# Values of the whole-key branches step by step, from a ring of three steps of turned weights

## The chip, the cores and the metric

The kernel runs on one core of a Trainium2 chip. The metric is device time in microseconds (us). The core has a matrix engine (TensorE, PE in the profile, its weight loads listed apart as PEld), VectorE (DVE), ScalarE (ACT), GpSimd (POOL), and a queue on SyncE (SP) that starts most transfers. The matrix engine writes to eight accumulation banks (`ps`) of 512 float32 values per partition.

## What is computed

One inference step of a two-layer decoder: an mLSTM layer, and then a sparse attention layer (NSA), for 512 prompt rows and for 8 sequences of 4 sample rows. The attention layer has three branches. In the first (compressed) the keys are few. The other two, selected and window, are computed in one stage here: for 512 positions and up to 16 blocks of 64 both see every key up to the query's own position, so they are ordinary causal attention over 512 keys, each with its own keys and values. Of the reference this is:

```python
    s = jnp.einsum('bqghd,bgqkd->bghqk', qg, kb) * scale
    p = _masked_softmax(s, (kpos <= qpos[None, None, :, None])[:, :, None])
    o_sel = jnp.einsum('bghqk,bgqkd->bqghd', p.astype(vb.dtype), vb)
    s = jnp.einsum('bqghd,bkgd->bghqk', qg, kwin) * scale
    wmask = ((wpos[None, :] <= qpos[:, None]) & (wpos[None, :] > qpos[:, None] - WINDOW)
             & (wpos[None, :] >= 0))
    p = _masked_softmax(s, wmask)
    o_win = jnp.einsum('bghqk,bkgd->bqghd', p.astype(vwin.dtype), vwin)
    o = jnp.stack([o_cmp, o_sel, o_win], axis=2)
...
    y = (o.astype(f32) * g[..., None]).reshape(bsz, s, 3, B_ATT) * jax.nn.silu(z.astype(f32))
    y = jnp.sum(y, axis=2).astype(x.dtype) @ w_out
```

There are 16 query heads in 4 key groups of 4 heads, 64 values wide.

## The kernel before, in words

The program is a row of stages; only `stage_keys` (the selected and the window branch, lines 2380 to 2763) is touched. Each engine has its own instruction list there, and they meet by semaphores only. `stage_out`, the output projection, follows.

**Units and pairs.** A unit (`units`, 16 of them) is one branch v, one half gp of the key groups and one tile i of 128 query rows. Within a half of units i runs 0, 1, 2, 3, and tile i sees i+1 key tiles of 128, so a unit with i = 3 costs four times one with i = 0. A unit has four pairs n = 4u + hh (64 in all); a pair is two heads (`par` 0 and 1) that belong to two key groups and sit in the upper and the lower half of the partitions.

**The loop.** Every engine runs over n. In iteration n PE computes the scores of pair n (line 2475) and adds the causal mask (2479); then, in some iterations, a part of the work for the sample rows (2488 to 2532), and up to iteration 59 a part of a gate projection of a later branch (`z_blocks`, line 2160, into bank 6); then it transposes the softmax weights of pair n-1 (2544, TURN = 1). DVE takes the maxima of the scores (2648), ACT the exponential with the row sum (2615), DVE the reciprocal times the branch gate (2673, 2674), and each of the two scales one head's weights (2677 on DVE, 2634 on ACT). `keep` copies the transposed weights of pair n-1 from their bank to the tile `PT` (2453 on DVE, 2451 on ACT). `gate` finishes a gate bank (2660).

**Values.** `PT` holds the turned weights of two whole units, [2, par, key tile, hh, 128]. When all four pairs of a unit are in it, three iterations after the last one's scores (`unit_at(n, TURN + 2)`, n = 4u + 6), PE computes the unit's output at once: for each key tile and each head half one matmul of 64 weight columns (the values V) with 512 moving columns (four pairs), at the end of the iteration (2556), in bank 7. One iteration later (n = 4u + 7) DVE multiplies it with the gate `z`, at the end of its iteration (`out`, 2686); GpSimd adds it to `y` (2762). `keep` waits, at a unit's first pair, for the values of the unit two before.

Of the kernel before, what the change touches and what calls it, by code (L numbers as in the profile page):

```python
# [15 lines left out]
T = 512  # L16
NT = T // 128
# [12 lines left out]
H, DH, G = 16, 64, 4  # L30
HPG = H // G
# [95 lines left out]
def open_at(pe, k, key, bank):  # L127

    n = k.bank_turns[bank]
    if n:  # L130
        pe.wait_ge(k.bank_free[bank], n)
    k.bank_turns[bank] = n + 1
    k.bank_of[key] = (bank, n + 1)
    return k.ps[:, bank], k.bank_full[bank]
# [9 lines left out]
def drained(eng, k, key):  # L144

    bank, n = k.bank_of[key]
    eng.wait_ge(k.bank_free[bank], n)
# [2229 lines left out]
def stage_keys(nc, k, ctx):  # L2377
# [5 lines left out]
    def sb(name, shape, dt=F32):  # L2383
        return ctx.enter_context(nc.sbuf_tensor(name, shape, dt))
    TURN = 1
    P = sb("P", [128, 2, 2, T])
    PT = sb("PT", [128, 2, 2, NT, HPG, 128])
    nmx = sb("nmx", [128, 4, 2])
    sm = sb("sm", [128, NT, H])
    rc = sb("rc", [128, 2, 2])  # L2390
# [12 lines left out]
    units = [(v, i, gp) for v in range(2) for gp in range(2) for i in range(NT)]  # L2403
    pairs = [(v, i, gp, hh) for v, i, gp in units for hh in range(HPG)]
    NP, NU = len(pairs), len(units)
# [30 lines left out]
    def unit_at(n, behind):  # L2436

        n -= behind
        return n // HPG if 0 <= n < NP and n % HPG == HPG - 1 else None

    def keep(eng, n, par):
        v, i, gp, hh = pairs[n]
        u = n // HPG
        if hh == 0 and u >= 2:
            bank, c = k.bank_of[("O", u - 2)]
            eng.wait_ge(k.bank_full[bank], c)
        b, free = full_bank(eng, k, ("T", n, par))
        dst = PT[:, u % 2, par, 0:i + 1, hh, :]
        src = b[:, 0:128 * (i + 1)].rearrange("p (j q) -> p j q", q=128)
        if par:  # L2450
            eng.activation(dst, src, ACT.Copy).then_inc(free, 1)
        else:
            eng.tensor_copy(dst, src).then_inc(free, 1)
# [10 lines left out]
    def _(pe):  # L2464
        z_features(pe, k, 1, 0)
        for n in range(STEPS):
# [14 lines left out]
            for a in range(2):  # L2481
                q = two(n, KEYS[a])
# [55 lines left out]
            if TURN <= n < NP + TURN:  # L2538
                i = pairs[n - TURN][1]
                for par in range(2):  # L2540
# [2 lines left out]
                    for j in range(i + 1):  # L2543
                        m = pe.transpose(b[:, 128 * j:128 * j + 128], P[:, (n - TURN) % 2, par, 128 * j:128 * j + 128], k.ident[:, :])
                    m.then_inc(full, 1)
            u = unit_at(n, TURN + 2)
            if u is not None:
                v, i, gp = units[u]
                for hh in range(HPG):
                    for par in range(2):  # L2550
                        drained(pe, k, ("T", HPG * u + hh, par))
                b, full = open_at(pe, k, ("O", u), 7)
                for j in range(i + 1):
                    for par in range(2):
                        g = 2 * gp + par
                        m = pe.matmul(b[64 * par:64 * par + 64, :], k.V[:, v, j, DH * g:DH * g + DH],
                                      PT[:, u % 2, par, j, :, :].rearrange("p h q -> p (h q)"), start=j == 0, stop=j == i)
                m.then_inc(full, 1)

    @block.sync  # L2560
    def _(sp):
# [77 lines left out]
    def _(dve):  # L2639
# [56 lines left out]
        for n in range(STEPS + 1):  # L2696
            if n in ROWS_BACK:
                add_samples(dve, k, st, ROWS_BACK[n])
            if n < NP:
                maximum(n)  # L2700
            for a in range(2):
# [44 lines left out]
            if gates_done(n) is not None:  # L2746
                bank, no = gates_done(n)
                gate(*bank, no)
            u = unit_at(n, TURN + 3)
            if u is not None:  # L2750
                out(u)

    @block.gpsimd
    def _(pool):
# [127 lines left out]
def build(nc, a, outs):  # L2882

    k = Ctx()
    with ExitStack() as ctx:
        def sb(name, shape, dt=F32, where=ctx):
            return where.enter_context(nc.sbuf_tensor(name, shape, dt))

        def sem(name):
            return ctx.enter_context(nc.semaphore(name))  # L2890
# [109 lines left out]
        k.gate_exp = sem("gate_exp")  # L3000
        k.gt_halved = sem("gt_halved")
        k.gate_done = sem("gate_done")
        k.y_ready = sem("y_ready")
        k.rows_read = sem("rows_read")
        k.xu_high = sem("xu_high")
# [122 lines left out]
```

## Time and profile before

| | us |
|---|---|
| median of 3 runs | 1504.17 (1503.64 to 1505.37) |
| the profiled execution | 1504.39 |
| its span on the core | 1502.6 |
| PE busy | 1396.2 (93%) |
| DVE busy | 743.9 (50%) |
| ACT busy | 515.8 (34%) |
| `stage_keys` loop, scores of pair 0 to the last product | 1139.0 to 1439.7 |

The span is what lies between the first and the last instruction; the profiled execution's own time adds 1.8 us around it. Matmuls are pipelined: a matmul's recorded end is modelled and lies some way behind its last column, so busy time of PE counts more than the columns. Each float32 matmul stands in the trace as two records.

### The profile page before, as it was taken

The page shows a single profiled execution, that of the slowest core. Times are in us where ns is not written, and L with a number is a line of the kernel's source. Part 1 is how long each engine was busy: PE and PEld are TensorE (multiplying, and loading weights), DVE is VectorE, ACT ScalarE, POOL GpSimd, SP SyncE. Part 2 cuts the span into 40 slices and gives each one's busy share as a digit, 9 for nine tenths or more (in the row PEclk, how much of TensorE's full clock was granted, in tenths as well). Part 3 has the DMA queues.
Part 4 walks back from the last instruction along what each step waited for, and adds up shares of the span by engine and source line. Part 5 has one row for each costly group of instructions (what it writes and reads, how often), then busy time and mean ns, then how long its engine had stood idle before and what let it go on. Part 6 is the DMA issues. An engine that isn't in the chain of part 4 may idle for free. (4 is left out here: it accounts for less than half of the span.)

```text
span 1502.6 us, 24705 instructions
## 1 busy us (share of the span) xinstructions
PE 1396.2 (93%) x9357; PEld 1002.6 (67%) x9357; DVE 743.9 (50%) x1575; ACT 515.8 (34%) x1227; POOL 189.6 (13%) x231
## 2 busy tenths in 40 slices
PE   4899899999996699999799999999999999999978
PEld 4899655454542599777577999787666555555456
DVE  4676446676755732625633231005034656565646
ACT  5232524242421332423522231122104545454542
POOL 5221041313130100000110110100000000010020
PEclk9999999999998799999899999997999999999999
DMA  6431236767677522222443340011141314141221
GB/s 188 167 113 56 72 105 225 252 221 256 222 257 261 212 84 86 85 102 87 146 170 120 102 165 11 3 60 58 57 124 33 122 52 141 60 113 63 43 93 60
DMA packets 93835, 182.06 MB, mean 121 GB/s; under 512 B 10855, under 2 KB 24835, under 8 KB 92515
## 3 DMA queue, kind: packets, MB, share of 16 engines
q1 hardware_dynamic: 90998, 164.88, 33.4%
q0 software_dynamic: 2720, 15.60, 3.1%
q8 instruction: 76, 1.25, 0.3%
q14 instruction: 41, 0.34, 0.1%
HBM read 133.82 MB, written 54.95 MB: 126 GB/s over the span
## 5 line engine op out<-in xcount | busy, mean ns | idle before, releaser
L1022 DVE SCALAR_TENSOR_TENSOR wring<-wring,nbw,ps 128x512 f32<-128x512 f32 x128 | 86.9, 742 | 59.8 <-PE ps L673 59.7
L2160 PE MATMUL ps<-xnT,wring 128*64 128x256 f32 (+1 forms) x768 | 101.3, 400 | 1.9 <-DVEq L2662 1.7
L2615 ACT ACTIVATE P<-ps,nmx 128x128 f32<-128x128 f32 (+3 forms) x128 | 66.3, 522 | 95.4 <-DVE nmx L2648 95.4
L2142 PE MATMUL ps<-xnT,wring 128*64 128x256 f32 (+1 forms) x768 | 90.4, 398 | 1.3 <-PEq L2874 1.3
L1417 PE MATMUL ps<-wh,xl 128*128 128x512 f32 x224 | 88.1, 393 | 0.0
L416 PE MATMUL ps<-xuh,wuh 128*128 128x256 f32 (+1 forms) x256 | 77.6, 303 | 11.3 <-DVE wring_low L363 10.3
L1238 PE MATMUL ps<-xh,wh 128*128 128x256 f32 (+1 forms) x256 | 75.0, 293 | 7.2 <-DVE xl L1284 7.1
L2142 PEld LDWEIGHTS ps<-xnT,wring 128*64 128x64 f32 x768 | 59.0, 139 | 32.2 <-issue 3.8
L2648 DVE TENSOR_REDUCE nmx<-ps 128x1 f32<-128x128 f32 (+3 forms) x128 | 56.8, 486 | 47.0 <-PE ps L2479 40.8
L417 PE MATMUL ps<-xul,wuh 128*128 128x256 f32 (+1 forms) x256 | 76.3, 298 | 0.0
L418 PE MATMUL ps<-xuh,wring_low 128*128 128x256 f32 (+1 forms) x256 | 76.3, 298 | 0.0
L1239 PE MATMUL ps<-xl,wh 128*128 128x256 f32 (+1 forms) x256 | 74.3, 290 | 0.0
L1240 PE MATMUL ps<-xh,wl 128*128 128x256 f32 (+1 forms) x256 | 73.9, 289 | 0.0
L2160 PEld LDWEIGHTS ps<-xnT,wring 128*64 128x64 f32 x768 | 50.9, 136 | 31.9 <-issue 8.4
L1902 PE MATMUL ps<-cRh,cwh 128*128 128x384 f32 x192 | 67.5, 352 | 0.0
L1370 DVE TENSOR_TENSOR wring_low<-wring,wh 128x512 fp32r<-128x512 f32 x64 | 41.1, 687 | 53.2 <-PE ps L1381 53.2
L1903 PE MATMUL ps<-cRl,cwh 128*128 128x384 f32 x192 | 65.4, 341 | 0.0
L1904 PE MATMUL ps<-cRh,cwl 128*128 128x384 f32 x192 | 65.4, 340 | 0.0
L2066 PE MATMUL ps<-xnT,wring 128*128 128x256 f32 (+1 forms) x256 | 60.6, 401 | 2.2 <-PEq L3096 2.2
L416 PEld LDWEIGHTS ps<-xuh,wuh 128*128 128x128 f32 x256 | 51.3, 200 | 11.8 <-issue 5.3
L2762 POOL TENSOR_TENSOR arena<-arena,tmp 128x512 f32<-128x512 f32 x16 | 20.3, 1271 | 303.5 <-DVEq L2689 303.5
L2066 PEld LDWEIGHTS ps<-xnT,wring 128*128 128x128 f32 x256 | 49.7, 195 | 12.8 <-issue 2.3
(489 smaller groups left out, 3135.3 us busy)
## 6 DMA issues: line engine op xcount, KB each, us to landing
wring<-in_state_C_dram SPq DMA_DIRECT2D x64, 512.0 KB, 5.2
out_dram<-wring SPq DMA_DIRECT2D x64, 512.0 KB, 5.3
wring<-in_a_w_up_dram SPq DMA_DIRECT2D x8, 2048.0 KB, 8.6
wring<-in_b_w_in_dram SPq DMA_DIRECT2D x8, 2048.0 KB, 9.1
wring<-in_a_w_down_dram SPq DMA_DIRECT2D x4, 2048.0 KB, 8.6
craw<-in_cache_kv_dram SPq DMA_DIRECT2D x64, 128.0 KB
arena<-in_cache_kv_dram SPq DMA_DIRECT2D x32, 256.0 KB, 3.9
arena<-in_cache_win_dram SPq DMA_DIRECT2D x8, 1024.0 KB, 6.0
```

The lines of the kernel that those rows point to most:

```text
L416: pe.matmul(b[:, 0:t1 - t0], w_hi, x_hi, start=kt == 0, stop=False)
L417: pe.matmul(b[:, 0:t1 - t0], w_hi, x_lo, start=False, stop=False)
L418: m = pe.matmul(b[:, 0:t1 - t0], w_lo, x_hi, start=False, stop=kt == KD - 1)
L1022: dve.scalar_tensor_tensor(out=c, in0=c, scalar=nbws[:, h % 2, 2 * S + s:2 * S + s + 1], in1=b[:, :], op0=ALU.mult, op1=ALU.add).then_inc( ...
L1238: pe.matmul(out, w_hi, x_hi, start=kt == 0, stop=False)
L1239: pe.matmul(out, w_hi, x_lo, start=False, stop=False)
L1240: m = pe.matmul(out, w_lo, x_hi, start=False, stop=kt == KD - 1)
L1417: m = pe.matmul(b, x_lo, w_hi, start=False, stop=last and kt == KD - 1)
L1902: pe.matmul(b[:, 0:CROW], w_hi, r_hi, start=j == 0, stop=False)
L2066: m = pe.matmul(b[:, 0:t1 - t0], w[:, kt, 128 * m4:128 * m4 + 128], k.xnT[:, kt, t0:t1], start=kt == 0, stop=kt == KD - 1)
L2142: m = pe.matmul(b[64 * par:64 * par + 64, 0:t1 - t0], w[:, kt, x:x + DH], k.xnT[:, kt, t0:t1], start=kt == 0, stop=kt == KD - 1)
L2160: m = pe.matmul(k.ps[64 * par:64 * par + 64, bank, 0:t1 - t0], w[:, kt, x:x + DH], k.xnT[:, kt, t0:t1], start=kt == 0, stop=kt == KD - 1)
```

## The change

`PT` becomes a ring of three pairs, [3, par, 512], written in one run. The values of pair n-3 are computed at the end of PE's iteration n, for that pair's heads alone: per key tile and half one matmul with 128 moving columns, into that pair's quarter of bank 7. The bank is opened at a unit's first pair and handed over at its last; for the three others a new semaphore `values_done` counts. `keep` now waits, for each pair n from 3 on, for the values of pair n-3. `out` moves from the end of DVE's iteration 4u + 7 to its start, ahead of the maxima.

```diff
--- before.py
+++ after.py
@@ -2384,7 +2384,8 @@
         return ctx.enter_context(nc.sbuf_tensor(name, shape, dt))
     TURN = 1
     P = sb("P", [128, 2, 2, T])
-    PT = sb("PT", [128, 2, 2, NT, HPG, 128])
+    SLOTS = TURN + 2
+    PT = sb("PT", [128, SLOTS, 2, T])
     nmx = sb("nmx", [128, 4, 2])
     sm = sb("sm", [128, NT, H])
     rc = sb("rc", [128, 2, 2])
@@ -2439,14 +2440,17 @@
         return n // HPG if 0 <= n < NP and n % HPG == HPG - 1 else None
 
     def keep(eng, n, par):
-        v, i, gp, hh = pairs[n]
-        u = n // HPG
-        if hh == 0 and u >= 2:
-            bank, c = k.bank_of[("O", u - 2)]
-            eng.wait_ge(k.bank_full[bank], c)
+
+        i = pairs[n][1]
+        if n >= SLOTS:
+            u, hh = divmod(n - SLOTS, HPG)
+            if hh == HPG - 1:
+                bank, c = k.bank_of[("O", u)]
+                eng.wait_ge(k.bank_full[bank], c)
+            else:
+                eng.wait_ge(k.values_done, (HPG - 1) * u + hh + 1)
         b, free = full_bank(eng, k, ("T", n, par))
-        dst = PT[:, u % 2, par, 0:i + 1, hh, :]
-        src = b[:, 0:128 * (i + 1)].rearrange("p (j q) -> p j q", q=128)
+        dst, src = PT[:, n % SLOTS, par, 0:128 * (i + 1)], b[:, 0:128 * (i + 1)]
         if par:
             eng.activation(dst, src, ACT.Copy).then_inc(free, 1)
         else:
@@ -2543,19 +2547,19 @@
                     for j in range(i + 1):
                         m = pe.transpose(b[:, 128 * j:128 * j + 128], P[:, (n - TURN) % 2, par, 128 * j:128 * j + 128], k.ident[:, :])
                     m.then_inc(full, 1)
-            u = unit_at(n, TURN + 2)
-            if u is not None:
-                v, i, gp = units[u]
-                for hh in range(HPG):
-                    for par in range(2):
-                        drained(pe, k, ("T", HPG * u + hh, par))
-                b, full = open_at(pe, k, ("O", u), 7)
+            if 0 <= n - TURN - 2 < NP:
+                o = n - TURN - 2
+                v, i, gp, hh = pairs[o]
+                if hh == 0:
+                    open_at(pe, k, ("O", o // HPG), 7)
+                for par in range(2):
+                    drained(pe, k, ("T", o, par))
                 for j in range(i + 1):
                     for par in range(2):
                         g = 2 * gp + par
-                        m = pe.matmul(b[64 * par:64 * par + 64, :], k.V[:, v, j, DH * g:DH * g + DH],
-                                      PT[:, u % 2, par, j, :, :].rearrange("p h q -> p (h q)"), start=j == 0, stop=j == i)
-                m.then_inc(full, 1)
+                        m = pe.matmul(k.ps[64 * par:64 * par + 64, 7, 128 * hh:128 * hh + 128], k.V[:, v, j, DH * g:DH * g + DH],
+                                      PT[:, o % SLOTS, par, 128 * j:128 * j + 128], start=j == 0, stop=j == i)
+                m.then_inc(k.bank_full[7] if hh == HPG - 1 else k.values_done, 1)
 
     @block.sync
     def _(sp):
@@ -2696,6 +2700,9 @@
         for n in range(STEPS + 1):
             if n in ROWS_BACK:
                 add_samples(dve, k, st, ROWS_BACK[n])
+            u = unit_at(n, TURN + 3)
+            if u is not None:
+                out(u)
             if n < NP:
                 maximum(n)
             for a in range(2):
@@ -2746,9 +2753,6 @@
             if gates_done(n) is not None:
                 bank, no = gates_done(n)
                 gate(*bank, no)
-            u = unit_at(n, TURN + 3)
-            if u is not None:
-                out(u)
 
     @block.gpsimd
     def _(pool):
@@ -3000,6 +3004,7 @@
         k.gate_exp = sem("gate_exp")
         k.gt_halved = sem("gt_halved")
         k.gate_done = sem("gate_done")
+        k.values_done = sem("values_done")
         k.y_ready = sem("y_ready")
         k.rows_read = sem("rows_read")
         k.xu_high = sem("xu_high")
```

**PE, the end of the loop.** The rows of TensorE's list from the scores of pair 61 on; lines 2475, 2479, 2544 and 2556 of before are 2479, 2483, 2548 and 2560 of the changed file. `x` counts matmuls. Before:

```order
L2475 MATMUL ps<-KT,Qp 128x512 x2
L2479 MATMUL ps<-causb,identb 128x128 x2
L2544 MATMUL ps<-ident,P 128x128 x8
L2475 MATMUL ps<-KT,Qp 128x512 x2
L2479 MATMUL ps<-causb,identb 128x128 x2
L2544 MATMUL ps<-ident,P 128x128 x8
L2556 MATMUL ps<-PT,V 64x512 x6
L2475 MATMUL ps<-KT,Qp 128x512 x2
L2479 MATMUL ps<-causb,identb 128x128 x2
L2544 MATMUL ps<-ident,P 128x128 x16
L2556 MATMUL ps<-PT,V 64x512 x8
```

And now:

```order
L2479 MATMUL ps<-KT,Qp 128x512 x2
L2483 MATMUL ps<-causb,identb 128x128 x2
L2548 MATMUL ps<-ident,P 128x128 x8
L2560 MATMUL ps<-PT,V 64x128 x6
L2479 MATMUL ps<-KT,Qp 128x512 x2
L2483 MATMUL ps<-causb,identb 128x128 x2
L2548 MATMUL ps<-ident,P 128x128 x8
L2560 MATMUL ps<-PT,V 64x128 x8
L2548 MATMUL ps<-ident,P 128x128 x8
L2560 MATMUL ps<-PT,V 64x128 x24
```

Each iteration has its values behind the transposes; the last row of before, eight matmuls of 512 columns behind the last transposes, is now the 24 of pairs 61 to 63, and those of pair 60 stand before them. The same holds for every iteration from n = 3 on.

**DVE, the last four steps' `out`.** The product of unit 14 (2686, now 2690) and the maxima of pair 63 (2648, now 2652). Before:

```order
L2648 TENSOR_REDUCE nmx<-ps 128x1 x2
L2673 RECIPROCAL rc<-sm 128x2
L2674 TENSOR_TENSOR rc<-rc,gt 128x2
L2677 TENSOR_SCALAR P<-P,rc 128x512
L2453 COPY PT<-ps 128x4x128
L2686 TENSOR_TENSOR tmp<-ps,z 128x512
L2453 COPY PT<-ps 128x4x128
L2686 TENSOR_TENSOR tmp<-ps,z 128x512
```

And now:

```order
L2690 TENSOR_TENSOR tmp<-ps,z 128x512
L2652 TENSOR_REDUCE nmx<-ps 128x1 x2
L2677 RECIPROCAL rc<-sm 128x2
L2678 TENSOR_TENSOR rc<-rc,gt 128x2
L2681 TENSOR_SCALAR P<-P,rc 128x512
L2457 COPY PT<-ps 128x512 x2
L2690 TENSOR_TENSOR tmp<-ps,z 128x512
```

The product has moved from between the last two copies to ahead of the maxima.

## Rows read from the trace of the kernel before

**Rows 1.** Busy time (us, instructions) of the engines by stretch, granted clock, DMA

```profile
1139.00:1192.00 53.00, 52.77 (x514) 29.85 (x513) 34.10 (x104) 26.55 (x86) 1.72 (x2) 1.00 0.27 81
...
1361.00:1413.00 52.00, 51.89 (x431) 26.81 (x428) 32.77 (x100) 24.67 (x83) 3.81 (x3) 1.00 0.13 46
1413.00:1427.00 14.00, 11.43 (x97) 5.64 (x97) 10.11 (x27) 8.45 (x21) 1.27 (x1) 1.00 0.52 106
```

**Rows 2.** Timeline (start, duration in us), PE and PEld around a values group

```profile
1295.85 3.65 PE L2556 MATMUL ps<-PT,V 128*64 128x512 f32 x16
...
1296.33 0.14 PEld L2556 LDWEIGHTS ps<-PT,V 128*64 128x64 f32 x2 [0.29 <-issue]
...
1296.76 0.14 PEld L2556 LDWEIGHTS ps<-PT,V 128*64 128x64 f32 x2 [0.28 <-issue]
...
1299.43 0.49 PE L2475 MATMUL ps<-KT,Qp 64*128 64x128 f32 x4
1299.85 0.11 PEld L2479 LDWEIGHTS ps<-causb,identb 128*128 128x128 bf16 x2
```

**Rows 3.** The same view, transposes and the scores behind them

```profile
1310.33 0.66 PE L2544 MATMUL ps<-ident,P 128*128 128x128 f32 x4
...
1310.92 0.70 PE L2475 MATMUL ps<-KT,Qp 64*128 64x256 f32 x4
```

**Rows 4.** The same view, values of the sample rows, 32 weight columns each

```profile
1303.93 1.08 PE L2529 MATMUL ps<-arena 128*32 128x128 f32 x32
...
1304.94 0.42 PE L2532 MATMUL ps<-V,arena 32*32 32x128 f32 x8
```

**Rows 5.** The same view, the gate projection of step 30 behind its wait

```profile
1273.49 0.71 PE L2160 MATMUL ps<-xnT,wring 128*64 128x288 f32 x4 [1.06 <-DVEq L2662]
```

**Rows 6.** Waits from 1139 to 1440 us: total us, times, longest

```profile
PE ps L2160 <- DVEq L2662: 1.7, 3, 1.1
...
PE ps L2475 <- ACT P L2615: 1.5, 2, 1.0
```

**Rows 7.** Timeline of DVE around the product `out` of unit 13

```profile
1410.80 1.02 DVE L2648 TENSOR_REDUCE nmx<-ps 128x1 f32<-128x384 f32 x2 [2.65 <-PE ps L2479]
...
1415.05 0.69 DVE L2686 TENSOR_TENSOR tmp<-ps,z 128x512 f32<-128x512 f32 x1 [0.52 <-DVEq L2662]
1416.05 1.29 DVE L2648 TENSOR_REDUCE nmx<-ps 128x1 f32<-128x512 f32 x2 [0.31 <-DVE tmp L2686]
```

**Rows 8.** Timeline of the last steps, all engines

```profile
1417.70 1.13 PE L2475 MATMUL ps<-KT,Qp 64*128 64x512 f32 x4 [0.96 <-ACT P L2615]
...
1423.48 1.28 DVE L2648 TENSOR_REDUCE nmx<-ps 128x1 f32<-128x512 f32 x2
...
1426.78 1.13 PE L2475 MATMUL ps<-KT,Qp 64*128 64x512 f32 x4
...
1427.96 1.04 PE L2544 MATMUL ps<-ident,P 128*128 128x128 f32 x8
...
1428.10 1.29 DVE L2648 TENSOR_REDUCE nmx<-ps 128x1 f32<-128x512 f32 x2 [0.77 <-PE ps L2479]
...
1431.42 1.09 PE L2544 MATMUL ps<-ident,P 128*128 128x128 f32 x8 [2.41 <-DVE P L2677]
...
1432.55 0.60 ACT L2451 ACTIVATE PT<-ps 128x512 f32<-128x512 f32 x1 [0.52 <-PE ps L2544]
1432.80 0.69 DVE L2453 COPY PT<-ps 128x512 f32<-128x512 f32 x1 [0.24 <-DVE tmp L2686]
...
1433.84 5.07 PE L2556 MATMUL ps<-PT,V 128*64 128x512 f32 x16 [1.33 <-DVE PT L2453]
...
1439.05 0.69 DVE L2686 TENSOR_TENSOR tmp<-ps,z 128x512 f32<-128x512 f32 x1 [5.56 <-PE ps L2556]
```

**Rows 9.** Busy time by stretch as in rows 1, during the last values group

```profile
1434.00:1436.00 2.00, 2.00 (x6) 0.67 (x7) 0.00 (x0) 0.00 (x0) 0.12 (x1) 0.50 0.00 0
```

## Prediction

> **What bounds the kernel now.** I read four views in this order: the busy time by stretch, the timeline of TensorE's matmuls, the list of waits, and the timeline of all engines at the end of the loop. The stage `stage_keys` with its 64 steps (pair n = 0 to 63) runs from 1139 to 1441 us. From 1139 to 1413 TensorE (PE) is busy over 98% of each stretch, at a granted clock of 1.00, while VectorE (DVE) is busy about 62% [rows 1]. So in the first 60 steps every column and every pause of PE is paid. From 1413 to 1427 PE is busy 11.4 of 14 us [rows 1]: those steps (60 to 63, four key tiles each) carry no gate projections, and the chain maximum, exponential, reciprocal, scaling sets their pace. From 1427 on, the stage hangs on one chain: transposes of pair 63, their copies, the last values chunk, its product on DVE, and the sum on GpSimd.
>
> One caution: a matmul's recorded duration holds some 0.17 us behind its last column, so I price PE work from start to start.
>
> **Part 1, four times as many values groups.** Before, one group per four steps: in step 34 it starts at 1295.85 and the scores behind it at 1299.43, 3.58 us [rows 2]. It is 16 records, two at a time (the two halves of 64 columns run together); a pair of records follows the last after 0.43 us (1296.33 to 1296.76), so the streaming is 8 x 0.427 = 3.41 us. The rest, 0.17 us, is a fixed price: the first pair takes 0.48 in place of 0.43 (0.05, weights that nothing hides), and about 0.10 to 0.12 passes at the change to the next shape. The transposes show the same: 4 records of 0.107 us are 0.43, the next shape starts 0.59 later, so 0.16 [rows 3]. I take 0.15 per group, bounds 0.14 and 0.17.
>
> Now there are 64 groups in place of 16. Each new one stands between transposes and scores, two shapes that already meet there with one change; it adds a change and a first load. Those of pairs 0 to 55 come before the scores of step 59, the last step that PE bounds: 56 against 14, so 42 x 0.15 = **+6.3 us** (5.9 to 7.1). The six left fall into the stretch where PE waits, and cost nothing as long as it does.
>
> Streaming itself: four matmuls of 128 columns in place of one of 512 are the same columns. What is not shown is 64-wide weights with 128 columns. The nearest row is narrower, values of the sample rows, 32 records, four at a time, 128 columns each: 8 x 0.107 = 0.85, and 1.01 passes to the next shape [rows 4], which leaves 0.15 or 0.16 fixed and nothing per pair. The scores of one key tile load two weights of 128 columns for each pair of 128 moving columns; their two pairs and both fixed parts take 0.42 (1299.43 to the mask matmuls at 1299.85) [rows 2]: 0.21 streaming, 0.10 first load, 0.10 change. They load twice as much per pair as the new groups and still hide the second pair's load. So 0 per pair.
>
> **Part 2, pauses of PE in the first 60 steps.** There are seven, where PE catches up with DVE or ScalarE: five times the gate projection waits until DVE has emptied its bank (the largest ends at 1273.49, [rows 5]), twice scores wait for a free bank. The waits list gives 1.7 us for the first kind and 1.5 for the second, of which 0.96 belongs to step 61 [rows 6, 8]; with 0.1 to 0.17 us hidden behind each previous matmul's recorded end, the seven are 2.9 us. Each lies in a step without a values group. Now each such step gets 0.36 us (one key tile) to 1.0 us (four), which pushes PE's need back while DVE's readiness stays, or comes earlier by the product `out` that no longer stands at an iteration's end. The 1.1 us pause keeps some 0.3. Against that, the steps before an old group lose the long break in which DVE caught up; where a group of three key tiles had stood (steps 14 and 46), DVE starts the maxima up to 0.7 us behind the scores, and the next gate projection may wait 0.2. I keep 0.6 us of pauses: **-2.3 us** (-2.9 to -1.4).
>
> **Part 3, the end.** In steps 60 to 63 PE needs 1.2 (scores and mask, 1426.78 to 1427.96) + 0.96 (transposes) + 1.0 (values) = 3.2 us a step, DVE 4.62 - 0.77 idle = 3.85 between the maxima of 62 and 63 [rows 8]. So DVE sets the pace. One `out` costs it 1.0 us, 1415.05 to 1416.05 with the pause behind it [rows 7]. Unit 13's moves ahead of the maxima of step 59, where DVE waits 2.65 us for scores [rows 7]: -0.7 from step 60 on (more is cut off by the scores of step 60). Unit 14's moves ahead of the maxima of 63, where 0.77 us was idle: +0.25. Transposes of pair 63 start 0.4 us earlier, at 1431.0 in the old count. Then, before: copies to 1433.5 (ScalarE's from 1432.55, DVE's from 1432.80, late because `out` stood ahead of it), the whole unit's values from 1433.84, recorded 5.07 us, its product at 1439.05 [rows 8]. Now: transposes until 1431.95, pairs 61 and 62 until 1433.95 while the copies of 63 run, pair 63 until 1434.85, and 0.2 to the product: 1435.05, **-4.0 us**.
>
> The clock: the old last group ran partly at 1.2 GHz (granted 0.50 from 1434 to 1436, [rows 9]) after PE had been idle 2.4 and 1.3 us with one group between [rows 8]; that cost it 5.07 - 3.65 = 1.4 us against step 34's [rows 2]. The new end still has about 2.2 us idle ahead of the last transposes, then none. Bounds 0 and 1.7; I take **+0.5**.
>
> Nothing else costs. The copies move as many elements, written in one run in place of strided; both a copy and the product of 512 elements take 0.69 us [rows 7, 8], so layout is not what limits them. The new wait of `keep` for pair n asks for the values of n-3, which PE has issued ahead of the transposes that `keep` waits for anyway. The first group of unit u now waits for `out` of u-1 at the start of the same DVE iteration; PE has scores, gate projection and transposes (over 2 us) ahead of it, so it is cover, until step 63. GpSimd's sums and what follows only shift.
>
> **Sum.** 6.3 - 2.3 - 4.0 + 0.5 = **+0.5 us**. The profiled execution took 1504.39 us, of which 1502.6 are its span; it lies 0.2 above the median of three, 1504.17. So the median becomes 1504.7. By the bounds it is -1.0 (5.9 - 2.9 - 4.0) to +3.4 (7.1 - 1.4 - 4.0 + 1.7), so 1503.2 to 1507.6.
>
> **Rivals.** (a) *Slower: DVE becomes the bound inside the loop.* Bank 7 opens for unit u only after `out` of u-1, and `out` delays the maxima of the same step by up to 0.5 us where the scores are short. If DVE runs more than 2 us behind PE at a unit's first step, PE waits there, some 0.4 us in each of 15 units: +6, 1510.7. Against: DVE waited for scores at those steps in the timeline, 2.65 us at step 59 [rows 7], and the old group's time is given to DVE in pieces, not taken. It decides from a lag of about 2 us. Chance 0.13. (b) *Slower: each weight load is paid.* If the 0.05 us of the first pair falls on every pair, 240 more pairs cost 12 us: 1516. The row of four at a time speaks against it [rows 4]. Chance 0.04. (c) *Faster: no price for the change of shape*, if small groups slip into the pauses behind transposes: only first loads, 42 x 0.05 = 2.1, so -3.7: 1500.5. Against: both the long and the short group pay it [rows 2, 3]. Chance 0.05. (d) *The end is not shortened*, because the chunk was not what the end waited for: +4.5, 1508.7. Against: DVE's 5.6 us wait for it ends at 1439.05 [rows 8]. Chance 0.04.
>
> The Trainium skill, page "TensorE: Matmul & The Clock Gate", section "The mechanism", says that a weight load overlaps running matmuls only where the row group differs. Here all groups use all 128 rows, so by that rule (b) would hold and the change would be 12 us slower; the rows of this trace disagree, since pairs in one row group follow each other at the pure streaming time.
>
> **Chances.** Forecast 0.74, (a) 0.13, (b) 0.04, (c) 0.05, (d) 0.04. 0.2% (3 us) is about what a measurement of this kernel can tell from no change. Faster by more: (c) and a little of the forecast, 0.07. Slower by more: (a), (b), (d) and the forecast's upper edge (above 1507.2), 0.23. Within: 0.70. The range of 8 in 10 is the forecast's, opened on both sides to the nearer part of (c) and (a): 1501.5 to 1509.
>
> **What would show it.** Right: 64 values groups, each about 0.15 us more than its streaming (0.36 us for one key tile, 1.0 for four); the scores of step 59 some 4 us later than 1409.69; the last product about 4.5 us after the last transposes start, against 7.6; PE's waits for DVE in the loop under 1 us. Wrong: pairs of 128 columns further apart than 0.11 us; waits of PE for `out` (bank 7); or maxima that start later than the scores by more than 1 us in most steps.

## The result

The changed kernel takes 1509.48 us (median of 8 runs, 1506.17 to 1513.38), the kernel before 1504.1 (8 runs, 1503.22 to 1506.19). The ratio is 1.0033, 95% interval 1.0019 to 1.0048: 0.2 to 0.5% slower. The forecast was 1504.7, with a range of 1501.5 to 1509.

The profiled execution of the changed kernel is the slowest of its eight, 1513.38 us; the head of its page:

```profile
span 1511.6 us, 25759 instructions
...
PEclk9899999999997899999899999988999999999979
```

I read both traces by four marks. All times are starts in the timeline, counted from the first scores of the loop (1139.01 before, 1140.37 after; what lies ahead of them is the same program in both):

| us from the first scores | before | after | difference |
|---|---|---|---|
| scores of pair 59 | 270.68 | 276.55 | +5.87 |
| transposes of pair 63 | 292.41 | 298.32 | +5.91 |
| product of the last unit | 300.04 | 305.30 | +5.26 |
| from there to the end of the span | 63.58 | 65.96 | +2.38 |

So the loss is made in the first 59 steps, steps 59 to 63 add nothing, the end gives back 0.65 us in place of 4, and the output stage, whose program is the same, took 2.4 us more in this execution. Another 1.36 us of the 9.0 between the two spans lie ahead of the first scores, where the program is the same too. In the 14 profiled executions of this case the first scores stand between 1137.7 and 1142.7 us, whatever was changed behind them, so the whole time of a single execution says less than the marks do.

**The loop.** Busy time by stretch, the columns as in [rows 1]: TensorE is still full, and now nearly so in the stretch of steps 60 to 62 as well (14.67 of 15 us), where it was busy 11.43 of 14 us.

```profile
1140.40:1193.00 52.60, 52.60 (x520) 30.95 (x518) 33.76 (x103) 26.62 (x86) 2.54 (x2) 1.00 0.27 81
...
1362.00:1417.00 55.00, 54.55 (x529) 32.26 (x529) 33.39 (x101) 25.85 (x84) 3.82 (x3) 1.00 0.13 44
1417.00:1432.00 15.00, 14.67 (x155) 8.97 (x155) 11.19 (x28) 8.39 (x21) 1.27 (x1) 1.00 0.37 75
```

The values of one pair with four key tiles, in TensorE's timeline (the answer to [rows 2]), line 2560 being the values and 2479 the scores:

```profile
1217.35 1.09 PE L2560 MATMUL ps<-PT,V 128*64 128x128 f32 x16
1218.37 0.49 PE L2479 MATMUL ps<-KT,Qp 64*128 64x128 f32 x4
```

1.02 us pass, 8 x 0.107 = 0.85 of them streaming: 0.17 per group, what the group of 3.4 us had paid once per unit.

**Pauses.** Between the first scores and those of pair 59 I add up TensorE's gaps beyond the usual 0.1 us. Before they were seven and 2.95 us; now four, at steps 15 (0.31), 30 (0.32), 40 (0.84) and 55 (0.52), and 1.99 us, all ahead of the gate projection. The largest is at step 40, where there was none. The rows are DVE's product `out` of unit 8 (2690), the maxima of pair 39, an instruction of GpSimd for the sample rows (2205), DVE's reciprocal times the branch gate (2678), the gate of iteration 39 (2664), and TensorE's wait for it:

```profile
1319.43 0.69 DVE L2690 TENSOR_TENSOR tmp<-ps,z 128x512 f32<-128x512 f32 x1
...
1320.43 0.76 DVE L2652 TENSOR_REDUCE nmx<-ps 128x1 f32<-128x256 f32 x2 [0.31 <-DVE tmp L2690]
...
1321.76 1.89 POOL L2205 TENSOR_TENSOR osall<-osall,gt 32x1024 f32<-32x1024 f32 x1
...
1322.20 1.48 DVE L2678 TENSOR_TENSOR rc<-rc,gt 128x2 f32<-128x2 f32 x1
...
1324.52 0.41 DVE L2664 SCALAR_TENSOR_TENSOR z<-masks,ps 128x256 f32<-128x256 f32 x1
...
1325.14 0.65 PE L2160 MATMUL ps<-xnT,wring 128*64 128x256 f32 x4 [0.77 <-DVEq L2666]
```

`out` and the 0.31 us behind it take 1.0 us of DVE's time ahead of the maxima. The larger loss is the product of 2 columns at 1322.20: it takes 1.48 us where its median is 0.16, and ends 0.02 us after GpSimd's instruction does. In the kernel before it is the product of step 40 that is long (0.92 us, at 1322.91), and no pause of TensorE follows there. By an estimate from these rows, with the product at 0.16 us the gate would have been ready 1.3 us earlier, before TensorE asked for it, and step 40 would have had no pause. No run moves GpSimd's instruction alone; two runs that move `out` bear on it below.

**The end.** The timeline of all engines, the answer to [rows 8]:

```profile
1422.60 1.29 DVE L2652 TENSOR_REDUCE nmx<-ps 128x1 f32<-128x512 f32 x2 [0.71 <-PE ps L2483]
...
1426.85 1.29 DVE L2652 TENSOR_REDUCE nmx<-ps 128x1 f32<-128x512 f32 x2 [0.50 <-PE ps L2483]
...
1435.38 1.29 DVE L2652 TENSOR_REDUCE nmx<-ps 128x1 f32<-128x512 f32 x2 [0.31 <-DVE tmp L2690]
...
1438.69 1.97 PE L2548 MATMUL ps<-ident,P 128*128 128x128 f32 x8 [2.42 <-DVE P L2681]
...
1440.59 4.93 PE L2560 MATMUL ps<-PT,V 128*64 128x128 f32 x48
...
1445.67 0.69 DVE L2690 TENSOR_TENSOR tmp<-ps,z 128x512 f32<-128x512 f32 x1 [5.07 <-PE ps L2560]
```

DVE waits for the scores of pairs 60 and 61 (0.71, 0.50), which it had not done before. And the last transposes and values run at half clock (1.2 in place of 2.4 GHz), as the busy time by stretch tells (granted clock in the last column but two):

```profile
1440.00:1442.00 2.00, 2.00 (x18) 1.67 (x18) 0.60 (x1) 0.60 (x1) 0.00 (x0) 0.50 0.00 0
1442.00:1444.00 2.00, 2.00 (x22) 2.00 (x20) 0.00 (x0) 0.00 (x0) 0.00 (x0) 0.50 0.00 0
...
1450.00:1452.00 2.00, 1.42 (x4) 1.17 (x5) 2.00 (x4) 2.00 (x5) 0.00 (x0) 0.50 0.16 49
```

The last row is the start of the output stage, at half clock as well.

### The profile page after: what moved, and what is told of

Same layout as the page of the kernel before. It is cut to its first block and busy times, and to the rows that moved or that the text cites. A ratio compares the mean times of both kernels' runs of the same rounds, so it can differ in the third digit from the quotient of the medians.

```text
span 1511.6 us, 25759 instructions
## 1 busy us (share of the span) xinstructions
PE 1409.1 (93%) x9837; PEld 1031.0 (68%) x9837; DVE 744.2 (49%) x1575; ACT 516.1 (34%) x1227; POOL 189.6 (13%) x231
```

## The experiments

Theory after the comparison: (T1) the loop pays a fixed price per group, for the change of tile shape and the first loads; (T2) the end would be worth its gain if the clock held. The rival to T1 is that DVE, late with gates and `out`, sets the loop's time, or that short pairs pay each weight load; to T2, that the clock has no part in the difference.

**The group beside its own shape.**

```diff
             if gates_at(n) is not None:
                 bank, (k0, k1) = gates_at(n)
                 z_blocks(pe, k, *bank, k0, k1)
+            if 0 <= n - TURN - 2 < NP:
+                ...            (the values of pair n-3, moved up)
             if TURN <= n < NP + TURN:
                 ...            (the transposes of pair n-1)
-            if 0 <= n - TURN - 2 < NP:
-                ...
```

> The changed kernel with each pair's values group moved, on TensorE alone, from behind the transposes to just behind the gate projection, which also uses 64 weight columns. Theory (the change is slow because each of 42 more groups pays about 0.16 us for a change of tile shape and a first unhidden load, in a loop that TensorE bounds): in steps 3 to 59 the group then meets its own shape, so 57 groups lose 0.16 us, 9 us against the changed kernel; some of it comes back as pauses, so 6 to 9 us less than the changed kernel and 1 to 4 us less than before, 1500 to 1503. Rival 1 (the loop is slow because DVE is late with the gate banks and `out`, not by the price of groups): the groups' place changes nothing, 1507 to 1510. Rival 2 (each weight load of a 128-column pair is paid, wherever it stands): 1507 to 1510 as well, with pairs further apart than 0.11 us in the trace.

Measured: 1501.62 us (11 runs), ratio to before 0.9983 (0.9973 to 0.9992), some 8 us less than the changed kernel. Scores of pair 59 at 269.21 in place of 276.55, with pauses of 3.11 in place of 1.99 us: 8.46 us less work for TensorE, and 56 groups stand ahead of that mark, so 0.151 us each. The timeline shows gate projection, values (2552) and transposes (2561) of step 59:

```profile
1408.51 1.19 PE L2160 MATMUL ps<-xnT,wring 128*64 128x288 f32 x8
1409.53 0.82 PE L2552 MATMUL ps<-PT,V 128*64 128x128 f32 x12
1410.29 0.88 PE L2561 MATMUL ps<-ident,P 128*128 128x128 f32 x6
```

From values to transposes pass 0.76 us for three key tiles (6 x 0.107 = 0.64 streaming): only the one change of shape, 0.1, is left. T1 holds, its rivals fall. Of the lower work the pauses took back 1.1 us. Not all of the 8 us is the loop's: the edit also puts the values of pair 61 ahead of the last transposes, and the last product follows these after 3.00 us, where the changed kernel took 6.98, partly at half clock.

**The old unit beside its own shape.**

```diff
                 z_blocks(pe, k, *bank, k0, k1)
+            u = unit_at(n, TURN + 2)
+            if u is not None:
+                ...            (the unit's values, moved up)
             if TURN <= n < NP + TURN:
```

> The kernel before with its unit-wide values group moved behind the gate projection, ahead of the transposes; nothing else. Theory (price per change of shape): 14 of the 16 groups lose 0.16 us, 2.2 us less than before, 1501.5 to 1502.5. Rival (a late transpose of up to 3.5 us makes DVE and ScalarE late): pauses of TensorE appear in the next steps, same as before or up to 3 us slower.

Scores of pair 59 at 268.70 against 270.68, with pauses 0.15 us longer: 2.13 us for 14 groups, 0.152 each, the same price from the other kernel. But the time is 1506.39 us (11 runs), ratio 1.0005 (0.9996 to 1.0014): no gain. In the profiled execution, the longest of the 11 (1509.26), half-clock stretches at the end were twice as long as before (6.8 against 3.4 us, twice) and from the last product to the end passed 66.01 us against 63.58; its first scores stood 3.7 us later than before, ahead of anything that was changed. The loop's price is as expected; the total is not, and not for the rival's reason, since the pauses hardly grew. What took the gain back in the other executions is not shown.

**Only the last unit step by step.**

```diff
-            if u is not None:
+            if u is not None and u < NU - 1:
                 ...            (values of a whole unit)
+            o = n - TURN - 2
+            if NP - HPG <= o < NP:
+                ...            (values of pair o, 128 columns, into bank 7)
...
-            if u is not None:
+            if u is not None and u != NU - 2:
                 out(u)
+            if n == NP - 1:
+                out(NU - 2)    (ahead of the maxima of pair 63)
```

> The kernel before with only the last unit (pairs 60 to 63) valued step by step, 3 more groups in place of 48, and `out` of the unit ahead of it moved to the start of step 63. Theory of the prediction: the end is 4 us shorter at full clock, 1500 to 1501. Rival, after the changed kernel's trace (the last groups run at half clock because TensorE idles 2.6 us ahead of the last transposes): about 1 us shorter on average, 1502.5 to 1504, with a wider spread over the runs than before.

1502.14 us (11 runs), ratio 0.9982 (0.9973 to 0.9991). The loop is as before (270.66). The end in this execution ran at full clock:

```profile
1430.51 1.09 PE L2544 MATMUL ps<-ident,P 128*128 128x128 f32 x8 [1.53 <-DVE P L2692]
...
1431.53 2.84 PE L2570 MATMUL ps<-PT,V 128*64 128x128 f32 x48
...
1434.52 0.69 DVE L2701 TENSOR_TENSOR tmp<-ps,z 128x512 f32<-128x512 f32 x1 [2.62 <-PE ps L2570]
```

From last transposes to last product 4.01 us, the 4.05 of the prediction's sum, against 7.63. Over the runs it is 2 us, between the two expectations. Whether the clock fell at the end of the other executions is not known; 2 us is also what the end turns out to be worth at equal clock (2.2, below).

**`out` back to the iteration's end.**

```diff
-            u = unit_at(n, TURN + 3)
-            if u is not None:
-                out(u)
             if n < NP:
                 maximum(n)
             ...
             if gates_done(n) is not None:
                 bank, no = gates_done(n)
                 gate(*bank, no)
+            u = unit_at(n, TURN + 3)
+            if u is not None:
+                out(u)
```

> The changed kernel with `out` put back to the end of DVE's iteration. Theory: the ring needs the early `out`, because bank 7 opens for the next unit in the very step at whose end `out` now stands; TensorE then waits for a whole DVE iteration every fourth step, 1 to 2 us in each of 15 units, 15 to 30 us slower than the changed kernel (1524 to 1540), and waits for bank 7 show in the list of waits. Rival (DVE keeps close enough to TensorE, and the early `out`, which stands ahead of the maxima, costs more than it gives): the same as the changed kernel or up to 3 us faster.

1544.36 us (4 runs), ratio 1.0262 (1.0246 to 1.0278), 35 us above the changed kernel. The list of waits (us in total, times, longest) has what was not there:

```profile
PEld ps L2560 <- DVEq L2692: 32.3, 15, 4.2
PE ps L2560 <- DVEq L2692: 28.7, 15, 3.9
```

15 waits for bank 7, one per unit after the first, 2.1 us each. The direction is the theory's, the size above its range. So the move of `out` belongs to the ring: it is the price of opening bank 7 three steps earlier. The pauses ahead of the gate projection at steps 15, 30 and 55 are 0.32, 0.32 and 0.52 us here too, so the early `out` is not their cause. At step 40 the pause is 0.15 us in place of 0.84, and none of the products of line 2678 is long.

**Fillers: the clock held at the end.** Matmuls without use fill TensorE's idle time; the lots are shorter than the idle time.

```diff
+def keep_awake(pe, k, count):
+    for _ in range(count):
+        pe.matmul(k.ps[:, 6, 0:128], k.ident[:, :], k.ident[:, :], start=True, stop=True)
...
+            if n == NP:
+                drained(pe, k, ("z", 2, 7, 1))
+                keep_awake(pe, k, 10)
             if TURN <= n < NP + TURN:
...
+            if n == NP + TURN + 1:     (in the kernel before only)
+                keep_awake(pe, k, 5)
...
+        keep_awake(pe, k, 11)          (behind the loop)
...
+        keep_awake(pe, k, 9)           (stage_out, ahead of its first matmul)
         hv.tiles(pe, ("o", 0), CH_OUT, 0, True, True, True, outer=True, between={24: samples})
```

> The kernel before with matmuls that compute nothing of use (128 columns against the identity, into the idle gate bank) in TensorE's idle times at the end: 10 ahead of the transposes of pair 63, 5 ahead of the last values, 11 behind them, 9 at the start of the output stage; each lot is shorter than the idle time measured there. Theory (half clock after idle time is what blurs the end): the granted clock stays 1.00 through the end of the stage, the last values take 3.7 us in place of 5.1, the first matmuls of the output stage 1.3 us in all less; 2.5 to 3.5 us less than before, 1501 to 1502, with a narrower spread. Rival (the clock falls anyway, or the fillers delay the real work): same as before or slower.

> The changed kernel with the same fillers (10, none, 11, 9). Theory: with the clock held, the 24 last short matmuls take 2.7 us in place of 4.9 and the output stage starts at full clock, so 4 to 6 us less than the changed kernel, 1503.5 to 1505.5; what is left against the kernel before with fillers is the loop's 5.9 us less the 3.5 us that the end gives: 2 to 3 us. Rival (the change's cost lies in the loop alone and the clock has no part): 1509, and 5 us or more above the kernel before with fillers.

Before with fillers: 1501.55 us (9 runs), ratio 0.9976 (0.9966 to 0.9986). Changed with fillers: 1506.12 (11 runs), ratio 1.0008 (0.9998 to 1.0018). By the ratios both gain some 3.7 us, and between them lie 4.6 us, nearly the 5.4 without fillers. The kernel before came out as its theory had it; the changed one is above its theory's 1503.5 to 1505.5 and below the rival's 1509. In both profiled executions no half clock is left from the loop on, until the last microseconds, and the marks can be compared:

| us | before, fillers | changed, fillers | difference |
|---|---|---|---|
| scores of pair 59 | 270.69 | 276.55 | +5.86 |
| transposes of pair 63 | 292.42 | 298.33 | +5.91 |
| from there to the last product | 6.22 | 4.01 | -2.21 |
| to the end of the span | 62.32 | 62.29 | -0.03 |

That is +3.67 us; of the 0.9 us that the medians have more, 0.54 lie ahead of the first scores in the two profiled executions. The timelines of the last transposes, values and product, before and changed:

```profile
1431.63 1.10 PE L2552 MATMUL ps<-ident,P 128*128 128x128 f32 x8 [0.18 <-DVE P L2688]
...
1434.06 3.65 PE L2566 MATMUL ps<-PT,V 128*64 128x512 f32 x16 [0.21 <-issue]
...
1437.85 0.69 DVE L2697 TENSOR_TENSOR tmp<-ps,z 128x512 f32<-128x512 f32 x1 [4.15 <-PE ps L2566]
```

```profile
1438.08 1.09 PE L2556 MATMUL ps<-ident,P 128*128 128x128 f32 x8
...
1439.10 2.84 PE L2568 MATMUL ps<-PT,V 128*64 128x128 f32 x48
...
1442.09 0.69 DVE L2699 TENSOR_TENSOR tmp<-ps,z 128x512 f32<-128x512 f32 x1 [2.56 <-PE ps L2568]
```

The 4.93 us of the 48 records are 2.84, so the changed end does run at the length that the prediction gave it once the clock holds. But the old group also gains (5.07 to 3.65), so at equal clock the step-by-step end is worth 2.2 us, not 4; my expectation of 2 to 3 us between the two kernels had overlooked that. T2 falls: the clock is not what makes the change slower on average. In the profiled executions without fillers the difference behind the first scores is 7.6 us in place of 3.7, and the 4 us more lie in the end and the output stage, where the half-clock stretches are.

**Fillers behind the stage only** (11 and 9, in the kernel before, none ahead of the transposes).

```diff
+        drained(pe, k, ("z", 2, 7, 1))
+        keep_awake(pe, k, 11)
...
+        keep_awake(pe, k, 9)
         hv.tiles(pe, ("o", 0), CH_OUT, 0, True, True, True, outer=True, between={24: samples})
```

> The kernel before with fillers behind the last values and at the start of the output stage only (11 and 9). It splits what the fillers gave there, 2.7 us in the profiled runs. Theory (each half-clock stretch costs what its own matmuls lose): the last product stays 7.6 us behind the last transposes, and from it to the end 62.3 us pass in place of 63.6; 1.0 to 2.0 us less than before. Rival (the clock of the output stage hangs on the idle time ahead of the last transposes too): 63.6 us or more remain.

1505.45 us (11 runs), ratio 1.0002 (0.9993 to 1.0011): nothing, though the stage's start ran at full clock. In the profiled execution another half-clock stretch stood 20 us into the output stage (64.03 us from last product to end). The rival's number holds (63.6 us or more): fillers in these places alone did not pay. Its reason, the idle time ahead of the last transposes, is not tested by it, and why that stretch comes and goes stays open.

**The width alone.**

```diff
-                for j in range(i + 1):
-                    for par in range(2):
-                        g = 2 * gp + par
-                        m = pe.matmul(b[64 * par:64 * par + 64, :], k.V[:, v, j, DH * g:DH * g + DH],
-                                      PT[:, u % 2, par, j, :, :].rearrange("p h q -> p (h q)"), start=j == 0, stop=j == i)
+                for hh in range(HPG):
+                    for j in range(i + 1):
+                        for par in range(2):
+                            g = 2 * gp + par
+                            m = pe.matmul(b[64 * par:64 * par + 64, 128 * hh:128 * hh + 128], k.V[:, v, j, DH * g:DH * g + DH],
+                                          PT[:, u % 2, par, j, hh, :], start=j == 0, stop=j == i)
```

> The kernel before with each unit's values in four runs of 128 columns per key tile in place of one of 512, in one group and in the same place; only the width changes. Theory: from the first scores to those of pair 59 0.3 to 0.7 us more than the 270.7 us of before (0.0023 us for each of 320 pairs of records in place of 80). Rival (each weight load of a short pair is paid, 0.05 us): 12 us more. It measures the part of the changed kernel's loop that is neither the 42 fixed prices nor the pauses.

Scores of pair 59 at 271.17, 0.49 us more than before. One unit with four key tiles, now 64 records:

```profile
1295.35 3.71 PE L2557 MATMUL ps<-PT,V 128*64 128x128 f32 x64
1298.99 0.49 PE L2475 MATMUL ps<-KT,Qp 64*128 64x128 f32 x4
```

3.64 us against 3.58 [rows 2]. The weight loads hide. That settles the split of the loop: 276.55 - 270.68 = 5.87; pauses fell by 0.96, so the work grew by 6.83 us, of which 0.49 are the short matmuls and 6.34 = 42 x 0.151 the groups. (This kernel was run once, in 1508.01 us, with the long half-clock stretches at the end; the loop is what it was for.)

**`out` behind the maxima.**

```diff
-            u = unit_at(n, TURN + 3)
-            if u is not None:
-                out(u)
             if n < NP:
                 maximum(n)
+            u = unit_at(n, TURN + 3)
+            if u is not None:
+                out(u)
```

> The changed kernel with `out` of each unit behind the maxima of its step in place of ahead of them. Theory (the early `out` helps the end little because it stands ahead of the maxima of pair 63, a step in which DVE sets the pace): the last transposes start 0.7 to 1.0 us earlier after the first scores than in the changed kernel (298.3 us), and the pauses of TensorE in steps 0 to 58, 2.0 us, fall to 1 us, since gates come no later and exponentials earlier; 1 to 2 us less than the changed kernel. Rival (bank 7 then comes free too late for the next unit): pauses ahead of the values groups, same or slower.

1508.44 us (11 runs), ratio 1.0023 (1.0014 to 1.0032), against the changed kernel's 1.0033 (1.0019 to 1.0048): not told apart. The marks contradict the theory: pauses 2.97 us in place of 1.99, scores of pair 59 at 277.54, last transposes at 299.16, 0.84 later. The pauses at steps 15, 30 and 55 are unchanged (0.32, 0.32, 0.52); step 40 alone went from 0.84 to 1.82, which is the whole difference. There two instructions of DVE are long, the product and the scaling of the weights (2681, 0.35 us otherwise), beside two of GpSimd:

```profile
1319.48 1.27 POOL L2766 TENSOR_TENSOR arena<-arena,tmp 128x512 f32<-128x512 f32 x1 [15.09 <-DVEq L2693]
...
1319.73 1.04 DVE L2678 TENSOR_TENSOR rc<-rc,gt 128x2 f32<-128x2 f32 x1
...
1320.83 1.89 POOL L2205 TENSOR_TENSOR osall<-osall,gt 32x1024 f32<-32x1024 f32 x1
...
1320.92 1.96 DVE L2681 TENSOR_SCALAR P<-P,rc 128x256 f32<-128x256 f32 x1
```

GpSimd's sum starts some 0.3 us behind the end of `out`. With `out` ahead of the maxima it falls on the maxima, which keep their time; with `out` behind them it falls on the product. In this run 15 of the 64 products take 0.22 to 1.04 us in place of 0.16, against one in the changed kernel, and each ends 0.02 us after an instruction of GpSimd. The one of pair 63 takes 1.00 us, ahead of the last transposes, so the 0.7 to 1.0 us that the theory had for the end were lost there.

**What the parts give together.** The kernel before with its units beside the gate projection (as in the second experiment, units 0 to 14) and the last unit step by step (as in the third), first without and then with fillers (10, 11, 9):

> Two parts put together that gained apart or in part: the kernel before, its unit-wide groups behind the gate projection for units 0 to 14, and the last unit step by step. Theory (the prices add): 2.0 us from the loop and 3.5 us from the end, 1499 to 1501 where the output stage's clock spells are as before. Rival (the longer pause ahead of the transposes feeds into the end, or the clock spells of the output stage become longer as in the run with the unit beside the gate): 1502 to 1504.

> The same with the fillers (10, none, 11, 9). Theory: 2 to 3 us less again, 1496.5 to 1498.5, and a spread under 3 us. Rival: as without fillers.

Without fillers 1501.66 us (8 runs), ratio 0.9977 (0.9965 to 0.999); with them 1496.55 (5 runs), ratio 0.9944 (0.993 to 0.9958), the fastest of all. The marks with fillers: pair 59 at 268.76, last product at 294.65 (before 270.68 and 300.04), 62.31 us behind it. Without fillers the time is 0.7 us above the theory's range; with them it is at its lower edge, though the spread, 4.0 us, is wider than the 3 expected. At held clock the two gains add: against the kernel before with fillers the last product comes 3.99 us earlier, 1.93 from the loop and 2.06 from the end.

Last, pair 61's values ahead of the last transposes with 4 fillers, and `out` of unit 14 behind the maxima of 63:

```diff
+                last_values(n - TURN - 2)      (at n == NP, ahead of the transposes)
-                keep_awake(pe, k, 10)
+                keep_awake(pe, k, 4)
...
-            if n == NP - 1:
-                out(NU - 2)
             if n < NP:
                 maximum(n)
+            if n == NP - 1:
+                out(NU - 2)
```

> The mixed kernel with fillers, and two steps more: values of pair 61 ahead of the transposes of pair 63 (in TensorE's idle time, in place of 6 of the 10 fillers), and `out` of unit 14 behind the maxima of pair 63. Theory: the last product comes 3.1 us behind the last transposes in place of 4.0, and these come 0.7 us earlier: 1.5 us less than mixed with fillers, 1495. Rival (`out` behind the maxima makes pair 60's values late, and they the last transposes): no gain, 1496.5.

1499.45 us (5 runs), ratio 0.9964 (0.995 to 0.9977). That is above the theory and the rival. The last product is at 294.28, 0.37 us earlier than in the kernel it builds on, but the last transposes are at 291.20, 0.56 later. In the timeline 2482 are the values, 2793 GpSimd's sum, 2703 DVE's product, 2379 the fillers and 2583 the transposes:

```profile
1429.39 1.97 PE L2482 MATMUL ps<-PT,V 128*64 128x128 f32 x32 [1.35 <-DVEq L2717]
1429.57 1.27 POOL L2793 TENSOR_TENSOR arena<-arena,tmp 128x512 f32<-128x512 f32 x1 [12.11 <-DVEq L2718]
...
1429.86 1.00 DVE L2703 TENSOR_TENSOR rc<-rc,gt 128x2 f32<-128x2 f32 x1
...
1431.28 1.16 PE L2379 MATMUL ps<-ident 128*128 128x128 f32 x8
...
1432.28 1.04 PE L2583 MATMUL ps<-ident,P 128*128 128x128 f32 x8
```

Pair 60's values wait 1.35 us for bank 7, and the fillers behind them now stand in the transposes' way: the rival's mechanism is there. The product again takes 1.00 us in place of 0.16 beside GpSimd's sum, which delays the weights that the transposes wait for; which of the two costs how much is not separated. Whether this kernel is slower than the one without those two steps is not settled: they ran on different chips, their intervals overlap, and in the profiled execution 1.2 us more lie ahead of the first scores. Both beat both kernels of the case.

## Why the prediction was wrong

The forecast was +0.5 us, and the medians differ by 5.4. What bounds the kernel in the first 60 steps was read rightly, and so was the price of a group. Three steps failed. The pauses fell by 0.96 us, not by 2.3, since DVE's readiness was taken as unchanged or earlier. Steps 60 and 61 were taken as paced by DVE, and the gain of 0.4 there was lost. And the end was priced against an old group at partly half clock: forecast -4.0, +0.5 for the clock, measured -2.2 at held clock and -0.65 in the profiled executions. At held clock the change costs 3.67 us by the marks, 4.6 by the medians. By its parts, with the clock held in both kernels:

| step | forecast | measured | miss |
|---|---|---|---|
| 42 groups and short matmuls | +6.3 | +6.83 | +0.5 |
| pauses filled | -2.3 | -0.96 | +1.3 |
| DVE earlier in steps 59 to 63 | -0.4 | 0.0 | +0.4 |
| last transposes to last product, with the clock's share | -3.1 | -2.2 | +0.9 |
| sum | +0.5 | +3.67 | |

- **The price per group** was right: 0.15 taken, 0.151 and 0.152 measured in two kernels. That streaming is the same was nearly so: 0.49 us for the short matmuls, which I had set to 0.
- **Pauses** were mis-sized. I kept 0.6 us of 2.9; 2.0 stayed. Two places I had named, 15 and 30, came (0.31, 0.32), the one behind step 46 did not; step 40 with 0.84 and step 55 with 0.52 (0.18 before) I had missed, and together they make up the miss. The step "DVE's readiness stays, or comes earlier by the product `out`" failed. At step 40 the rows show why: the product of the reciprocals took 1.48 us in place of 0.16 beside an instruction of GpSimd, a term that my sum did not have; its part is read from the rows and from the two runs with `out` elsewhere (0.15 and 1.82 us), not tested by itself. At step 55 the pause is the same wherever `out` stands, so `out` is not its cause; that DVE had caught up during the old groups is likely and not shown.
- **DVE sets the pace from step 60 on** was wrong for steps 60 and 61. I summed TensorE's step without the sample rows' values of step 60, and DVE waited 0.71 and 0.50 us for scores there. The earlier `out` did bring the maxima of pair 60 forward by 0.7 us (5.68 us behind the scores of pair 59 in place of 6.36), but those of pair 61 then waited for TensorE, and 0.6 of it was lost; the groups of pairs 57 and 58 were not free.
- **The end** failed on a comparison of unlike clocks. The old last group had run partly at 1.2 GHz, 5.07 against 3.65 us; I set it against a new end at full clock and added only 0.5 for the risk. Held at full clock in both, the end is worth 2.2 us. Without fillers it was worth 0.65 in the profiled executions, but that is no equal clock either: the half-clock stretch was 3.4 us long in the old end and 6.8 in the new.
- **Behind the stage** I had nothing: "GpSimd's sums and what follows only shift". The output stage took 2.4 us more in the profiled execution by longer half-clock stretches. How many executions have that is not known; with fillers the difference is -0.03.
- **Rivals.** (b) and (c) fell: loads hide, the change of shape is paid. The numbers of (a), 1510.7, and (d), 1508.7, are nearer to 1509.5 than the forecast, by luck: neither came for its reason. (a) named DVE's lag, but its form was wrong: in the changed kernel bank 7 is hardly waited for (0.2 us, ahead of pair 60's values), the gate banks are. Where `out` comes late the mechanism is real: 15 waits, 32 us. (d) had the end unshortened because nothing waited for the last group; the last product still waits 5.07 us for it.
- **What no part explains:** of the 5.4 us between the medians, the marks at held clock give 3.67. The rest lies ahead of the loop and in the half-clock stretches of single executions, and no run settles how it is shared.
- The page "TensorE: Matmul & The Clock Gate" of the Trainium skill, section "The mechanism", whose rule on weight loads stood behind (b), disagrees with the runs here as well: the width alone cost 0.49 us where (b) had 12.

## What to carry to other kernels

On an engine that is full, cut work into pieces only where a piece stands beside work of the same tile shape: here the same groups cost 0.15 us less each behind the gate projection than behind the transposes, and that one move turned 5 us slower into 2.6 us faster. Take the finer cut only where something waits for it, at the end of the loop. And before counting a gain on a stretch that ran at half clock, price both kernels' stretch at the same clock. Where DVE sets a step's pace, look at what GpSimd runs beside it: moving `out` by one place decided whether GpSimd's sum fell on the maxima, which kept their time, or on a product of 2 columns, which then took up to 1.04 us in place of 0.16.

## What the hardware showed that I had not expected

- The clock at the end takes more than one form. In the profiled execution of the width alone (last transposes at 292.96 against 292.41) there were half-clock stretches of 6.8 us twice, and one more of 3.4 in the output stage, where the kernel before had 3.4 twice; 1.4 us more from last transposes to product and 2.4 behind it. In the five profiled executions with a stretch of 6.8 us near the start of the output stage (changed, unit beside gate, width alone, group beside gate, `out` back) the part behind the last product took 65.96 to 66.68 us, in the four with one of 3.4 there (before, last unit step by step, `out` behind the maxima, the parts together) 63.58 to 63.81. One execution of each kernel was profiled, so whether the edit or chance chose the form is not shown.
- A short product on DVE with two operands (`rc` and `gt`) did not end while GpSimd's instruction beside it ran: 0.92 us in the kernel before, 1.48 in the changed one, 0.22 to 1.04 in 15 cases of the run with `out` behind the maxima, each ending 0.02 us after GpSimd. In that run 15 reciprocals of one operand started beside GpSimd's instructions too, and took 0.14 to 0.17 us, their usual time.
- Matmuls without use gained some 3.6 us in the kernel before when placed ahead of the last transposes, ahead of the last values and behind them (35 in all), and nothing when only the 20 behind were kept.
